# Where a two-block transformer kernel sums its squares, makes T3 and T4, and updates X

## The reference, cut to what matters

```
n = rms_norm(h, g)                    # h * rsqrt(mean(h*h) + eps) * g
h = h + 0.5 * ((silu(n @ w_gate) * (n @ w_up)) @ w_down)
...                                   # the mixer: h = h + mixed @ w_out
n = rms_norm(h, g2); h = h + 0.5 * swiglu(n, ...)
```

## Time and profile before

| | us |
|---|---|
| median of 3 runs | 2490.89 (2489.54 to 2491.67) |
| the profiled execution, own time | 2488.78 |
| its span | 2486.8 |
| PE busy | 2440.2 (98%) |
| DVE busy | 1705.4 (69%) |
| ACT busy | 1081.3 (43%) |

### The profile page before, as it was taken

How to read it: one execution, slowest core, us unless ns; L and a number is a source line. 1 busy time by engine, 2 the same in 40 slices (tenths; PEclk the granted TensorE clock), 3 DMA queues, 4 the chain that set the end, 5 groups by cost and what they waited for, 6 DMA issues and landing times.

```text
span 2486.8 us, 49060 instructions
## 1 busy us (share of the span) xinstructions
PE 2440.2 (98%) x20460; PEld 2245.9 (90%) x20460; DVE 1705.4 (69%) x2926; ACT 1081.3 (43%) x1959; POOL 98.2 (4%) x108
## 2 busy tenths in 40 slices
PE   9999999999999999999999999999989999999998
PEld 7999999996887989898999999898867888989896
DVE  6878675646656879688879684242976445879694
ACT  5444343334434535356535253112874324535352
POOL 0000001000320000001000002000000000000001
PEclk8999999999999999998999999999999999999999
DMA  4233333220001333332233333232212333233322
GB/s 148 85 107 102 102 95 90 81 80 11 4 13 44 103 111 98 107 103 85 73 115 106 99 93 97 71 93 76 55 48 76 92 96 101 100 102 103 102 90 72
DMA packets 72379, 213.01 MB, mean 86 GB/s; under 512 B 12796, under 2 KB 20028, under 8 KB 72032
## 3 DMA queue, kind: packets, MB, share of 16 engines
q1 hardware_dynamic: 70496, 209.03, 26.7%
q0 software_dynamic: 480, 0.73, 0.1%
q10 hardware_dynamic: 1184, 0.12, 0.0%
HBM read 207.61 MB, written 2.20 MB: 84 GB/s over the span
## 4 chain that ended last, share of the span: by engine, by line
PE 87%; DVE 7%; ACT 4%; issue 2%; DVEq 0%; POOL 0%; ACTq 0%; POOLq 0%
PE PS L863 21%; PE PS L1398 20%; PE PS L1355 11%; PE PS L1356 11%; PE PS L1357 11%; DVE WL L948 1%; PE PS L1233 1%; ACT WH L936 1%; PE PS L1706 1%; PE PS L1707 1%; PE PS L1705 1%; PE PS L1319 1%; PE PS L2256 1%; DVE P L2888 1%; PE PS L2825 1%
## 5 line engine op out<-in xcount | busy, mean ns | idle before, releaser
L1355 PE MATMUL PS<-OPH,WH 128*128 128x256 f32 (+1 forms) x2112 | 606.4, 287 | 3.1 <-DVE OPL L1105 2.7
L1357 PE MATMUL PS<-OPH,WL 128*128 128x256 f32 (+1 forms) x2112 | 601.8, 285 | 0.0
L1356 PE MATMUL PS<-OPL,WH 128*128 128x256 f32 (+1 forms) x2112 | 600.2, 284 | 0.0
L936 ACT ACTIVATE WH<-WR 128x1024 fp32r<-128x1024 f32 (+2 forms) x277 | 275.5, 995 | 564.0 <-PE PS L863 272.6
L948 DVE TENSOR_TENSOR WL<-WR,WH 128x1024 fp32r<-128x1024 f32 (+2 forms) x277 | 318.7, 1151 | 191.1 <-ACT WH L936 191.0
L1355 PEld LDWEIGHTS PS<-OPH,WH 128*128 128x128 f32 x2112 | 403.5, 191 | 6.5 <-DVE OPL L1105 3.0
L1356 PEld LDWEIGHTS PS<-OPL,WH 128*128 128x128 f32 x2112 | 403.5, 191 | 2.1 <-issue 1.7
L1357 PEld LDWEIGHTS PS<-OPH,WL 128*128 128x128 f32 x2112 | 402.7, 191 | 0.0
L936 ACT ACTIVATE WH<-SUMS 128x512 fp32r<-128x512 f32 x352 | 211.1, 623 | 229.8 <-DVE SUMS L974 186.6
L948 DVE TENSOR_TENSOR WL<-SUMS,WH 128x512 fp32r<-128x512 f32 x352 | 234.1, 684 | 21.5 <-ACT WH L936 21.2
L863 PE MATMUL PS<-NHI,WH 128*128 128x264 f32 (+2 forms) x960 | 234.5, 309 | 1.5 <-ACT TMP L2623 1.0
(11 more groups left out here) (472 smaller groups left out, 4670.3 us busy)
## 6 DMA issues: line engine op xcount, KB each, us to landing
WR<-in_ffn_up SPq DMA_DIRECT2D x64, 512.0 KB, 3.9
WR<-in_ffn_down SPq DMA_DIRECT2D x64, 512.0 KB, 3.7
WR<-in_ffn_gate SPq DMA_DIRECT2D x56, 512.0 KB, 3.7
WR_MORE<-in_ffn_gate SPq DMA_DIRECT2D x32, 512.0 KB, 4.5
WR_MORE<-in_ffn_up SPq DMA_DIRECT2D x24, 512.0 KB, 4.4
WR<-in_ffn_down SPq DMA_DIRECT2D x32, 384.0 KB, 3.3
WR<-in_w_gate SPq DMA_DIRECT2D x24, 512.0 KB, 3.6
WR<-in_w_out SPq DMA_DIRECT2D x16, 512.0 KB, 3.6
```

Source lines behind the costliest of these rows:

```text
L936: e.activation(split_unit(i)[0][:, 0:w], src, ACT.Copy).then_inc(S["w_hi"], 1)
L1355: e.matmul(o, wh[:, at:at + 128], hi, start=k == 0 and s in (1, 2, 5), stop=False, skip_group_check=True)
L1356: e.matmul(o, wh[:, at:at + 128], lo, start=False, stop=False, skip_group_check=True)
L1357: last = e.matmul(o, wl[:, at:at + 128], hi, start=False, stop=k == 3, skip_group_check=True)
```

## The change

Three things change in code; the same matmuls are computed, but for three fillers that are left out.

1. `pe_sums_after` loses most of its sums. For f = 0 they go between the groups of p1 and p2 (`pe_sums_inside`), with fewer fillers. For f = 1 and 3 the `ACC` sum goes behind w_out's product 5, the sum of tile 4 behind product 6 and that of tile 5 behind product 7; tile 6 stands behind p5 and tile 7 behind p2. For f = 2 the sum of `ACC_2` and `ACC` goes behind w_down's product 4 and opens the group.
2. T3 and T4 of groups 1 and 2 (and the split of T3) leave the tile loop and join group 3 behind it, in f = 1, 2 and 3.
3. In `dve_out` the update of X comes ahead of the weight splits of the same m.

```diff
@@ act_operands
-            if f and i:
-                act_third(e, q, f, i - 1)
+            if f and i == 1:
+                act_third(e, q, f, 0)
@@ act_late_operands
-                act_third(e, q, f, 3)
+                for i in range(1, 4):
+                    act_third(e, q, f, i)
@@ dve_operands
-            if f and i:
-                dve_third(e, q, f, i - 1)
+            if f and i == 1:
+                dve_third(e, q, f, 0)
...
-            if f and i > 1:
-                dve_third_low(e, q, f, i - 2)
@@ dve_late_operands
-                dve_third(e, q, f, 3)
-                dve_third_low(e, q, f, 2)
+                for i in range(1, 4):
+                    dve_third(e, q, f, i)
+                    dve_third_low(e, q, f, i - 1)
@@ pe_square_sums
-                q.wait_ge(*free[1])
+                q.wait_ge(*(free[1] if f < 3 else ("w_added", DT + 5)))
@@
+        def pe_sums_opened(e, q, f):
+            if f == 2:
+                q.wait_ge("acc", acc_after(3, 3))
+            elif f:
+                q.wait_ge("acc", acc_after(FFN[f][5], ADDED_BY_POOL[f][-1]))
+            else:
+                q.wait_ge("sq", 1)
+            pe_square_sums(e, q, f, None, 0, opens=True)
@@ pe_sums_after
-            if f == 1 and step in (("down", 2, DT - 2), ("down", 2, DT - 1)):
-                pe_square_sums(e, q, 2, TMP, step[2] - 2, opens=step[2] == DT - 2)
-            if step == ("p", 0, 1):
-                if f == 0:
-                    q.wait_ge("sq", 1)
-                    pe_square_sums(e, q, f, None, 0, opens=True)
-                    for k in range(1, 3):
-                        pe_square_sums(e, q, f, TMP, k)
-                elif f != 2:
-                    q.wait_ge("acc", ACC_BASE[FFN[f][5]] + 3)
-                    pe_square_sums(e, q, f, None, 0, opens=True)
-            if step == ("p", 0, 5):
-                if f == 2:
-                    q.wait_ge("acc", acc_after(4, 3))
-                    q.wait_ge("meta_acc", 1)
-                    pe_square_sums(e, q, f, None, 0)
-                if f == 0:
-                    pe_square_sums(e, q, f, TMP, 3)
-                pe_square_sums(e, q, f, TMP, 6 if f == 2 else 4)
+            if f == 1 and step == ("down", 2, 4):
+                q.wait_ge("acc", acc_after(4, 3))
+                q.wait_ge("meta_acc", 1)
+                pe_square_sums(e, q, 2, None, 0, opens=True)
+            if f == 1 and step[:2] == ("down", 2) and step[2] in (6, 7):
+                pe_square_sums(e, q, 2, TMP, step[2] - 2)
+            if f == 0 and step == ("p", 0, 5):
+                pe_square_sums(e, q, f, TMP, 2)
+                pe_square_sums(e, q, f, TMP, 3)
+            if f > 0 and step == ("p", 0, 5):
+                pe_square_sums(e, q, f, TMP, 6)
             if step == ("p", 0, 2):
-                for k in range(7 if f == 2 else 5, DT):
-                    pe_square_sums(e, q, f, TMP, k)
+                pe_square_sums(e, q, f, TMP, 7)
+
+        def pe_sums_inside(e, q, s, k):
+            if s == 1 and k == 2:
+                pe_sums_opened(e, q, 0)
+                pe_filler(e, q, 1)
+            if s == 1 and k == 3:
+                pe_square_sums(e, q, 0, TMP, 1)
+                pe_filler(e, q, 1)
+            if s == 2 and k > 0:
+                pe_square_sums(e, q, 0, TMP, 3 + k)
+                if k > 1:
+                    pe_filler(e, q, 1)
@@ pe_step
-                    if f == 0 and k > (1 if s == 1 else 0):
-                        pe_filler(e, q, 2 if s == 1 else 1)
+                    if f == 0:
+                        pe_sums_inside(e, q, s, k)
@@ pe_out
+                f = 1 if name == "w_out" else 3
+                if m == 5:
+                    pe_sums_opened(e, q, f)
+                for k in range(ADDED_BY_POOL[f][-1] + 1, 6):
+                    if m == 7 if k == 5 else m == 6:
+                        pe_square_sums(e, q, f, TMP, k)
@@ dve_out
+                q.wait_ge("w_used", DONE[name, m])
+                e.tensor_tensor(X[:, m, NM:L], PS[:, out_bank(name, m), 0:SEQ], X[:, m, NM:L],
+                                ALU.add).then_inc(S["w_added"], 1)
                 if name != "w_out":
                     dve_split(e, q, U[name, m] + 2)
                 if name == "w_out" or m == DT - 1:
                     dve_split(e, q, U[name, m] + 3)
-                q.wait_ge("w_used", DONE[name, m])
-                e.tensor_tensor(X[:, m, NM:L], PS[:, out_bank(name, m), 0:SEQ], X[:, m, NM:L],
-                                ALU.add).then_inc(S["w_added"], 1)
```

## The result

The changed kernel takes 2497.41 us (median, 2494.66 to 2499.91) against 2489.54 (2484.70 to 2492.07) for the kernel before: ratio 1.0033, 95% interval 1.0023 to 1.0043, so 8.2 us slower (interval 5.7 to 10.7). The forecast was 2496.7: 5.8 us more than the kernel before, whose median stood at 2490.89 over the three runs known then. The profiled execution took 2497.16 with a span of 2495.2, close to the median.

The account below looks back on a forecast made before the run. PE works nearly all the span, so time was to be had only in its waits and at lower clock. Head terms -1.0 - 3.6 + 4.5 + 5.9 = +5.8 us gave 2494.6 on the profile's scale, 2496.7 as median, range 2486 to 2503.5.

Parts of the forecast that it names:

- The step that failed: Ahead of p7, PE waits for the copy of p6: 3.3 us at f = 1, 3.8 at f = 2, 6 at f = 3.
- The chain: Update of X tile 7 to copy of p6: 1.85 us longer (2.1 at f = 2), another 1.15 at f = 3.
- chain not binding: Rival at the heads: DVE and ACT make up the 1.85 us, p7 starts when PE arrives; -12.6 us, 2478, chance 0.08.
- POOL: Behind w_down's product 4, ahead of the f = 2 sums: PE waits 3.2 us for POOL's last additions.
- POOL is in time: Rival at head f = 2: POOL's third pair ends before product 4; total +0.1 us, 2491, chance 0.17.
- The clock: Half-clock costs behind new waits at heads f = 1, 2 and 3: four terms, 7.7 us together.
- +5.9: Head f = 3: p7 3.9 us later plus 2.0 of clock; range +3.9 to +7.3 us.
- +4.5: Head f = 2: p7 0.5 us later plus 2.5 and 1.5 of clock; range +0.5 to +7.7 us.
- -3.6: Head f = 1: p7 5.35 us sooner, less 1.7 of clock; range -5.3 to -2 us.
- the clock stays up: Rival at the heads: spread sums and new waits leave the clock alone; -3.9 us, 2487, chance 0.13.
- worse: Rival: every wait brings a half-clock stretch of 10 us or more; +13 us, 2504, chance 0.12.
- f = 0: Head f = 0: copy of p6 stays at 43.86, p7 comes sooner; -1.0 us, range -3 to 0.

Follow-up runs that it names:

- e4: Changed kernel with ACT's copy of p1 moved ahead of the splits of T3 and T4, for f = 1 to 3: 2497.18 us.
- e1: Changed kernel with T3 and T4 of groups 1 and 2 back in the tile loop: 2488.22 us.
- e11: Changed kernel with only the last X update of w_out_2 (m = 7) behind its SUMS and splits again: 2493.18 us.
- e10: Kernel before with only the f = 2 sums of ACC_2 and ACC moved behind w_down's product 4: 2492.02 us.
- e12: Changed kernel with the f = 2 sums of ACC_2 and ACC behind w_down's product 5 instead of 4: 2490.70 us.
- e7: Kernel before with only the sums of f = 0 moved between the groups of p1 and p2: 2489.05 us.
- e5: Kernel before with only T3 and T4 of groups 1 and 2, and the splits of T3, moved behind the tile loop: 2493.20 us.
- run 33: A count, not a label: the kernel before, unchanged, was run 33 times beside e10 to e13, from 2485.85 to 2495.77 us.
- e13: Kernel before with X updated ahead of the weight splits everywhere but at the last product of w_out_2: 2483.95 us.
- e2: Changed kernel with the f = 2 sums of ACC_2 and ACC back behind p5 of f = 2: 2493.85 us.
- e3: Changed kernel with T3 and T4 back in the tile loop and the f = 2 sums back behind p5: 2485.00 us.

## Why the prediction was right, and where it was not

**Where PE waits.** The step that failed is that PE stands ahead of p7 of block 0, for the copy of p6. In the changed kernel p6 waits for the copy of p1, by 3.00, 1.81 and 4.18 us at f = 1, 2 and 3, and takes up nearly all that p7 would have waited. What the prediction read in the kernel before is there, but small (timeline of PE; the last matmul ahead of p7 and the first of p7):

```profile
2137.04 0.28 PE L1357 MATMUL PS<-OPH,WL 128*128 128x256 f32 x1
2137.45 0.39 PE L1355 MATMUL PS<-OPH,WH 128*128 128x256 f32 x1
```

They start 0.41 us apart, where neighbours start 0.12 apart, so PE stood for 0.3 us. The view names no releaser, but p7 starts 0.43 us behind the start of the copy of p6, exactly as in the changed kernel (2144.91 and 2145.34). That trace shows no wait ahead of p6, and the prediction didn't ask what p6 needs. The error cost nothing in time, since both copies hang on the same list of DVE and ACT (e4: the wait moves, the time doesn't). At f = 3 the forecast wait of 6 us is 4.18 ahead of p6 and 1.7 of lower clock between p6 and p7 (6.1 us instead of 4.4), 5.9 together.

**The chain.** From the update of X tile 7 to the start of the copy of p6 the prediction's terms come to 14.05 us at f = 1, 16.5 at f = 2 and 16.6 at f = 3. The profile has 14.05 (802.95 to 817.00), 16.4 (1163.94 to 1180.37) and 16.66 (2128.25 to 2144.91). The lengths, counted from single instructions, were right within 0.1 us. e1 and e11 confirm 1.85 and 1.15 by taking them away (waits of 3.00 and 4.18 become 1.14 and 2.32; 4.18 becomes 3.00). The rival "chain not binding" fell with them.

**POOL.** Forecast 3.2 us, measured 2.98, and 3.03 and 3.04 in e1 and e10. The rival that POOL is in time fell. e12 shows that one product later it would have been.

**The clock** is the mis-sized term. I took 1.7 at f = 1, 2.5 and 1.5 at f = 2, 2.0 at f = 3: 7.7 us. At p7 the start behind the copy, less the 0.43 us in which it could follow, is 819.68 - 817.43 = 2.25 at f = 1, 1181.63 - 1180.80 = 0.83 at f = 2, and 2145.34 - 2145.34 = 0 at f = 3; behind product 4 half of 3.4, 1.7. Together 4.8. At f = 3 the stretch of 3.4 us is there, but it falls in the time in which PE would have waited for the copy of p6 anyway (as in e1, 1.56 us). That brings f = 3 from +5.9 to +4.2, f = 2 from +4.5 to +3.2, and f = 1 from -3.6 to -2.7. The rivals "the clock stays up" and "worse" both fell.

**f = 0**: -1.7 in the profile for -1.0 forecast; e7 alone gives -1.0 (-3.2 to +1.2) and can't tell it from nothing. That the copy of p6 stays at 43.86 was wrong, it starts at 45.04. The lower level lasts 17.1 us in this piece before and after, so the spread sums spared no clock.

**What the sum left out.** That the medians agree to 0.7 us is partly luck. The forecast of the difference, 5.8, is 2.4 us short of the 8.2, and more than half of that is hidden because the kernel before stood 1.4 us higher over its first three runs. In the profiles the heads give only +3.0. The other 4.9 us stand in stages that no part touches. Windows of PE from the wait for HROOT to w_out's product 3, before, and then after:

```profile
748.43:768.33 19.90, 18.75 (x101) 1.00 0.00 1
```

```profile
749.77:772.92 23.15, 22.00 (x100) 0.85 0.00 1
```

The same matmuls (101 and 100 of them recorded) behind the same wait (1.67 us before, 1.66 after) run through at full clock in one and not in the other. This is chance between runs: up to w3, e5 and e10 have the very instructions of the kernel before, and there the same piece takes 23.15 and 21.55 us. Over the 14 profiles of this study the piece from the spread of f = 0 to w3 takes 719.60 to 725.93 us, and the profile of before has the lowest value. The mean is 723.6 for the eight kernels with the sums inside f = 0 and 723.1 for the six without, so that part of the change costs nothing there. The piece from spread f = 2 to N takes 696.22 to 701.02. The same kernel before, run 33 times beside e10 to e13, went from 2485.85 to 2495.77.

That leaves the question of why the ratio says 8.2 us (5.7 to 10.7) when the heads of this profile hold 3.0. The idle time of PE answers most of it: 46.6 us in the profile before and 56.8 after, and 9.4 of these 10.2 us are in the heads. Against them stands clock time: in the heads the lower level lasts 47.8 us before and 37.5 after, but in the rest it lasts 31.5 and 41.8, so that the sum is 79.3 in both profiles. The runs say the same. Each has a span and a mean granted clock; one minus that clock, times the span, is 39.2 us in the mean of the 7 runs of the changed kernel, and 37.9 over the 92 runs of the kernel before that stand beside the experiments. The changed kernel thus saves no clock time on the whole. Without the saving that this one profile shows in its heads they would lose 3.0 + 10.3 / 2 = 8.1 us, an estimate, but one of the measured size. Whether in other runs the heads save none, or save it and the stages behind them lose it again, one profile per kernel can't tell.

**The parts don't add.** Alone they give +3.5, -7.7, -1.0, -0.5 and +3.0, in sum -2.7; together +8.2. T3 and T4 later cost 3.5 us alone and 9.9 in the company of the rest (by the ratios of e1 and of the change). Pieces of the profiles show where: alone they cost +1.1 at f = 1, +0.1 at f = 2, +1.7 at f = 3; with the rest +2.9, +2.9 and +1.9. The account that fits is that in the kernel before PE still had rows of sums to do while DVE worked at its list, and X tile 7 was late at f = 1 anyway; the other parts took both away, and the list lay bare. The waits ahead of p6 agree: with T3 and T4 later alone (e5) they are 1.61 us at f = 1, none at f = 2 and 0.87 at f = 3, in the changed kernel 3.00, 1.81 and 4.18. How much of the 9.9 is clock isn't separated. The forecast added up each head whole, with all parts in it, so it could come near the total without saying what any part costs alone.

## What to carry to other kernels

Work that is moved out of a loop to its end goes to the front of whatever waits for the last iteration: count what stands in each engine's list between the last input and the first copy that another engine waits for, and do it for every semaphore of that list, the earliest one first. Here the lengths of such chains could be forecast to 0.1 us from single instructions; what the clock does could not, so a change that lives on clock terms has to be run. Where one profile gives a change another size than the runs do, add up PE's idle time and its clock time apart, over the whole span. And before parts are bundled, each is worth a run alone: here the one edit that moved an update ahead of the splits was worth 7.7 us (4.7 to 10.7), and the four others, bundled with it, turned that into a loss of 8.

## What the runs showed of the hardware

Waits for semaphores repeat from kernel to kernel to a few hundredths: 3.00 us ahead of p6 of f = 1 in the changed kernel, e2, e11 and e12; 4.18 at f = 3 in the changed kernel, e2 and e12. The granted clock does not. Behind a wait of 1.14 us at f = 1 in e1 it was at the lower level for 3.4 us; behind 2.32 and 1.56 us at f = 3 in the same profile not at all. In e3 it was the other way round: at f = 1 no stretch behind the same 1.14 us, at f = 3 a stretch of 3.4 us behind the same 2.32. The Trainium skill (TensorE: Matmul & The Clock Gate, What's actually happening) says that idling brings the lower level back; the trace agrees that every new stretch in the heads has a wait or a row of one-column sums ahead of it, and adds that the length of one wait doesn't tell whether a stretch follows.
